# Second attention of a two-layer block: scores in three rounded products, probabilities scaled by GpSimd, one weight's low part later

## The reference

```python
sc = jnp.einsum('bkgqd,bksd->bkgqs', qb, k).astype(jnp.float32) * scale
pr = jax.nn.softmax(sc, axis=-1).astype(v.dtype)
return jnp.einsum('bkgqs,bksd->bkgqd', pr, v)
...
o = o.transpose(1, 0, 4, 2, 3, 5).reshape(b, s, MIX_WIDTH)
return (o * jax.nn.silu(gate)) @ w_out
```

## Time and profile before

| | us |
|---|---|
| median of 3 runs | 1265.69 (1264.97 to 1266.23) |
| profiled execution | 1264.7 |
| its span | 1262.9 |
| PE busy | 1153.4 (91%) |
| DVE busy | 629.2 (50%) |
| ACT busy | 509.6 (40%) |
| POOL busy | 414.4 (33%) |
| mean granted TensorE clock | 0.971 of full |

### The profile page before, as it was taken

How to read it: one execution, slowest core, us unless ns; L and a number is a source line. 1 busy time by engine, 2 the same in 40 slices (tenths; PEclk the granted TensorE clock), 3 DMA queues, 4 the chain that set the end, 5 groups by cost and what they waited for, 6 DMA issues and landing times.

```text
span 1262.9 us, 24765 instructions
## 1 busy us (share of the span) xinstructions
PE 1153.4 (91%) x10379; PEld 971.7 (77%) x10379; DVE 629.2 (50%) x1377; ACT 509.6 (40%) x1038; POOL 414.4 (33%) x214
## 2 busy tenths in 40 slices
PE   3999999999897999999998949987999799999996
PEld 3988887899897998565888949865777678678862
DVE  6000004833647169788246483117865766345546
ACT  4222225842324322788432363144863421132321
POOL 4644374873524344101434234122004441000000
PEclk9999999999899999999998979988999898999999
DMA  7433342232122223100321222431003222100001
GB/s 206 139 101 100 100 130 88 68 87 70 65 68 68 79 90 100 34 2 1 101 81 53 68 100 68 124 118 59 2 1 100 67 67 70 55 31 4 3 3 67
DMA packets 73177, 89.59 MB, mean 71 GB/s; under 512 B 1993, under 2 KB 66634, under 8 KB 72938
## 3 DMA queue, kind: packets, MB, share of 16 engines
q1 hardware_dynamic: 70136, 78.65, 19.5%
q0 software_dynamic: 2416, 8.26, 2.6%
q10 hardware_dynamic: 514, 1.11, 0.4%
HBM read 83.75 MB, written 4.26 MB: 70 GB/s over the span
## 4 chain that ended last, share of the span: by engine, by line
PE 72%; DVE 10%; issue 7%; ACT 5%; POOL 3%; DMA 2%; ACTq 0%; DVEq 0%; POOLq 0%
PE bank L468 67%; PE bank L736 2%; ACT arena L1277 1%; POOL ring_parts L2497 1%; PE bank L902 1%; DMA x<-x_kept 1%; PE bank L646 1%; DVE stat L1776 1%; DVE x L1943 1%; POOL arena L2617 1%; ACT ring_parts L1306 1%; DVE stat L1777 1%; DVE arena L1799 1%; DVE arena L1787 1%; DVE x L1796 1%
## 5 line engine op out<-in xcount | busy, mean ns | idle before, releaser
L2497 POOL TENSOR_TENSOR ring_parts<-ring,ring_parts 128x2048 fp32r<-128x2048 f32 (+1 forms) x59 | 268.4, 4550 | 368.0 <-ACT ring_parts L1306 367.8
L468 PE MATMUL bank<-ring_parts,hT_parts 128*128 128x256 f32 x1664 | 331.6, 285 | 18.9 <-DVE arena_parts L1810 10.8
L468 PE MATMUL bank<-hT_parts,ring_parts 128*128 128x512 f32 x896 | 290.2, 402 | 15.9 <-POOL ring_parts L2497 9.8
L468 PEld LDWEIGHTS bank<-ring_parts,hT_parts 128*128 128x128 f32 x1664 | 270.7, 193 | 20.7 <-issue 11.2
L1277 ACT ACTIVATE arena<-bank 128x512 f32<-128x512 f32 (+3 forms) x356 | 166.7, 527 | 270.7 <-PE bank L468 262.3
L468 PE MATMUL bank<-ring_parts,arena_parts 128*128 128x256 f32 x1088 | 257.0, 285 | 3.4 <-POOL hT_parts L2514 3.4
L468 PE MATMUL bank<-arena 64*64 64x64 f32 (+6 forms) x3440 | 217.6, 276 | 6.5 <-DVE x L2323 2.1
L468 PEld LDWEIGHTS bank<-hT_parts,ring_parts 128*128 128x128 f32 x896 | 173.3, 193 | 58.8 <-POOL ring_parts L2497 11.3
L468 PEld LDWEIGHTS bank<-arena 64*64 64x64 f32 (+2 forms) x3440 | 157.8, 142 | 59.4 <-issue 24.1
L468 PEld LDWEIGHTS bank<-ring_parts,arena_parts 128*128 128x128 f32 x1088 | 190.3, 192 | 4.3 <-POOL hT_parts L2514 3.8
L1306 ACT ACTIVATE ring_parts<-ring 128x2048 fp32r<-128x2048 f32 (+1 forms) x59 | 111.0, 1883 | 80.2 <-PE bank L468 80.2
(11 more groups left out here) (241 smaller groups left out, 1460.7 us busy)
## 6 DMA issues: line engine op xcount, KB each, us to landing
ring<-in_a_w_in SPq DMA_DIRECT2D x16, 1024.0 KB, 5.4
ring<-in_w_in SPq DMA_DIRECT2D x15, 1024.0 KB, 5.5
ring<-in_b_w_in SPq DMA_DIRECT2D x10, 1024.0 KB, 5.1
ring<-in_ple_w_gate SPq DMA_DIRECT2D x8, 1024.0 KB, 4.9
arena<-rpb_rows POOLq DMA_DIRECT2D x16, 256.0 KB, 3.4
ring<-in_a_w_out SPq DMA_DIRECT2D x4, 1024.0 KB, 5.0
ring<-in_b_w_out SPq DMA_DIRECT2D x4, 1024.0 KB, 5.0
ring<-in_w_out SPq DMA_DIRECT2D x4, 1024.0 KB, 5.2
```

What stands on the lines that cost most here:

```text
L468: return nc.tensor.matmul(o, l, r, start=start, stop=stop)
L2497: nc.gpsimd.tensor_tensor(rounded(r), r, read_back(high_slot(n)[:, 0:m]), ALU.subtract)\
```

## The change

- k's and q's transposed tiles become two parts. ScalarE writes the high part (rounded copy, B_high), VectorE then subtracts it from the PSUM bank to get the low part and frees the bank: 12 of them (4 of k, 8 of q). q's low parts go to hT, k's to kTB_lo, new in the arena.
- TensorE turns k's tiles first, then the first halves of q's; the second halves are turned behind scoresB(0), with their parts on ScalarE behind the exponentials of step 0 and on VectorE behind its reciprocals of step 0.
- scoresB issues three rounded products per tile and head, 12 matmuls of 64 rows x 512 columns for a step, the two heads in turn.
- VectorE makes the reciprocals only; GpSimd multiplies the tiles of pB by them (tensor_scalar, B_inverse and B_probs). Its low_pair(1, 0) to (1, 4) stand at the head of steps 6, 8, 10, 12 and 14.
- The low part of the second quarter of the output weights, BO 1, is made behind low_pair(1, 7).

```diff
-        arena = sb2("arena", [P, NARENA], (0, 12288), (19456, 6144))
+        arena = sb2("arena", [P, NARENA], (0, 12288), (19456, 8192))
...
+        kTB_lo = area(25600, 2048).rearrange("p (g t) -> p g t", g=4)
...
 # TensorE
-            for i in range(NT):
-                pe.wait_ge(S("B_rope"), i + 1)
+            def turn_kB(i):
                 pe.wait_ge(S("B_rope_k"), i + 1)
-                for hf in range(2):
-                    b = begin(("BqT", i, hf), "a")
-                    for q in range(4):
-                        o = (4 * hf + q) * P
-                        ins = nc.tensor.transpose(b[:, q * P:(q + 1) * P], qB[:, i, o:o + P], ident)
-                    end(ins)
-                b = begin(("BkT", i), "a")
+                b = begin(("BkT", i), "v")
                 for g in range(4):
                     ins = nc.tensor.transpose(b[:, g * P:(g + 1) * P], kD[:, i, g * P:(g + 1) * P], ident)
                 end(ins)
-            evacuated(pe, ("BkT", NT - 1))
+
+            def turn_qB(i, hf):
+                pe.wait_ge(S("B_rope"), i + 1)
+                b = begin(("BqT", i, hf), "v")
+                for q in range(4):
+                    o = (4 * hf + q) * P
+                    ins = nc.tensor.transpose(b[:, q * P:(q + 1) * P], qB[:, i, o:o + P], ident)
+                end(ins)
+
+            q_parts = [rounded(v[:, :, :]) for v in (qT, hT)]
+            k_parts = [rounded(v[:, :, :]) for v in (kTB, kTB_lo)]
 
             def scoresB(s):
 
-                for m in range(4):
-                    j, i, e = s // 2, 2 * (s % 2) + m // 2, 64 * (m % 2)
-                    b = begin(("BS", 4 * s + m), "a")
-                    end(mm(b[:, :], qT[e:e + 64, j, i * P:(i + 1) * P], kTB[e:e + 64, j // 2, :], True, True))
+                j = s // 2
+                if s == 0:
+                    evacuated(pe, ("BqT", NT - 1, 0))
+                if s == 8:
+                    evacuated(pe, ("BqT", NT - 1, 1))
+                for i in (2 * (s % 2), 2 * (s % 2) + 1):
+                    bs = [begin(("BS", 4 * s + 2 * (i % 2) + e), "a") for e in range(2)]
+                    last = [None, None]
+                    for a, c in ((0, 0), (0, 1), (1, 0)):
+                        for e in range(2):
+                            es = slice(64 * e, 64 * e + 64)
+                            last[e] = mm(bs[e][:, :], q_parts[a][es, j, i * P:(i + 1) * P], k_parts[c][es, j // 2, :],
+                                         (a, c) == (0, 0), a == 1)
+                    for ins in last:
+                        end(ins)
+
+            for i in range(NT):
+                turn_kB(i)
+            for i in range(NT):
+                turn_qB(i, 0)
...
             for s in range(16 + 2):
                 if s < 16:
                     scoresB(s)
+                if s == 0:
+                    for i in range(NT):
+                        turn_qB(i, 1)
 # ScalarE
+            def high_turned(key, dst):
+
+                b = take(act, key)
+                nc.scalar.activation(rounded(dst), b[:, :].rearrange("p (j t) -> p j t", j=4), ACT.Copy)\
+                    .then_inc(S("B_high"), 1)
...
             for i in range(NT):
-                for hf in range(2):
-                    key = ("BqT", i, hf)
-                    b = take(act, key)
-                    give(copy(qT[:, 4 * hf:4 * hf + 4, i * P:(i + 1) * P], b[:, :].rearrange("p (j t) -> p j t", j=4)), key)
-                key = ("BkT", i)
-                b = take(act, key)
-                give(copy(kTB[:, :, i * P:(i + 1) * P], b[:, :].rearrange("p (j t) -> p j t", j=4)), key)
+                high_turned(("BkT", i), kTB[:, :, i * P:(i + 1) * P])
+            for i in range(NT):
+                high_qB(i, 0)
...
+                if s == 0:
+                    for i in range(NT):
+                        high_qB(i, 1)
 # VectorE
+            def low_turned(key, dst, high):
+
+                turned_B[0] += 1
+                dve.wait_ge(S("B_high"), turned_B[0])
+                b = take(dve, key)
+                give(TT(rounded(dst), b[:, :].rearrange("p (j t) -> p j t", j=4), read_back(high), ALU.subtract), key)
...
+            for i in range(NT):
+                ts = slice(i * P, (i + 1) * P)
+                low_turned(("BkT", i), kTB_lo[:, :, ts], kTB[:, :, ts])
+            for i in range(NT):
+                low_qB(i, 0)
...
-                    link(nc.vector.reciprocal(stat[:, c + 8:c + 10], stat[:, c:c + 2]))
-                    for v in (u, u + 1):
-                        c = 144 + v % 8
-                        TS(pB[v % 8], pB[v % 8], stat[:, c:c + 1], None, ALU.mult).then_inc(S("B_probs"), 1)
+                    if u >= 8:
+                        dve.wait_ge(S("B_probs"), u - 6)
+                    nc.vector.reciprocal(stat[:, c + 8:c + 10], stat[:, c:c + 2]).then_inc(S("B_inverse"), 1)
+                if s == 0:
+                    for i in range(NT):
+                        low_qB(i, 1)
 # GpSimd
-                for j in range(2 if l == 0 else 0, 7):
+                for j in range(2 if l == 0 else 5, 7):
                     low_pair(l, j)
...
                 low_pair(l, 7)
+                lower(HI[("AO" if l == 0 else "BO", 1)])
                 if l == 0:
-                    lower(HI[("AO", 1)])
...
-                    lower(HI[("B", 1)], HI[("BO", 1)])
+                    lower(HI[("B", 1)], HI[("BO", 0)])
+                    for s in range(16):
+                        if s >= 6 and s % 2 == 0:
+                            low_pair(1, (s - 6) // 2)
+                        for u in range(4 * s, 4 * s + 4):
+                            pool.wait_ge(S("B_inverse"), u // 2 + 1)
+                            c = 144 + u % 8
+                            nc.gpsimd.tensor_scalar(pB[u % 8], pB[u % 8], stat[:, c:c + 1], None, ALU.mult)\
+                                .then_inc(S("B_probs"), 1)
```

More of the change, by code:

```diff
@@ L1488, in _, with high_qB @@
             high(HI[("BO", 1)])
-            for i in range(NT):
-                for hf in range(2):
-                    key = ("BqT", i, hf)
-                    b = take(act, key)
-                    give(copy(qT[:, 4 * hf:4 * hf + 4, i * P:(i + 1) * P], b[:, :].rearrange("p (j t) -> p j t", j=4)), key)
-                key = ("BkT", i)
-                b = take(act, key)
-                give(copy(kTB[:, :, i * P:(i + 1) * P], b[:, :].rearrange("p (j t) -> p j t", j=4)), key)
+            def high_turned(key, dst):
+                b = take(act, key)
+                nc.scalar.activation(rounded(dst), b[:, :].rearrange("p (j t) -> p j t", j=4), ACT.Copy)\
+                    .then_inc(S("B_high"), 1)
+            def high_qB(i, hf):
+                high_turned(("BqT", i, hf), qT[:, 4 * hf:4 * hf + 4, i * P:(i + 1) * P])
+            for i in range(NT):
+                high_turned(("BkT", i), kTB[:, :, i * P:(i + 1) * P])
+            for i in range(NT):
+                high_qB(i, 0)
             for s in range(16 + 2):
@@ L2021, in _, with low_qB @@
                 gates_B(2 * i + 1)
+            turned_B = [0]
+            def low_turned(key, dst, high):
[3 more added lines that the diff above has]
+                give(TT(rounded(dst), b[:, :].rearrange("p (j t) -> p j t", j=4), read_back(high), ALU.subtract), key)
+            def low_qB(i, hf):
+                at = (slice(None), slice(4 * hf, 4 * hf + 4), slice(i * P, (i + 1) * P))
+                low_turned(("BqT", i, hf), hT[at], qT[at])
+            for i in range(NT):
[3 more added lines that the diff above has]
+                low_qB(i, 0)
             def outB(s):
```

## The result

The changed kernel takes 1288.31 us in the median (1288.01 to 1288.99, 4 runs), the kernel before 1265.96 beside it: ratio 1.0177, 95% interval 1.0159 to 1.0195, 22 us slower. The forecast was 1263.5 us, no change that can be told, with a range of 1259.8 to 1271 us; the measured time lies far above it. The profiled execution took 1288.54 us, its span 1286.4.

A forecast was written before the change was run, and what follows sets the result against it. TensorE was taken to bound the second attention at 5.70 us a step. +1.6 (way in) - 3.8 (12 steps x 0.32) + 0 (way out) = -2.2 us gave 1263.5 us, range 1259.8 to 1271.

The forecast's parts named there:

- the price of GpSimd's scaling: Second attention's steps: one tensor_scalar on 512 columns takes 0.8 us, with 0.54 and 1.28 us as ends.
- rival 2: Second attention: GpSimd becomes the bound or the late one; 1271.5 us at 1.28 per scaling; chance 0.15, half of it slower.
- Products of two heads share the array: Score section of a step: rounded pairs run together, 6 slots of 0.233 us, 1.60 us instead of 1.92.
- The step without GpSimd's bound: Second attention: TensorE's transposes, values and scores, 1.90 + 1.87 + 1.60 = 5.37 us a step, where it was 5.70.
- ScalarE was not next: ScalarE's mean 5.05 us fits the step; the rival that it holds the step near 5.7, 1267.3 us, had chance 0.1.
- The weight's low part: Behind the stage on GpSimd: 4.64 us moved after the last low_pair, with 5 us of cover, costs nothing.
- the low_pairs at the heads of the steps: GpSimd's list in the second attention: five low_pairs, one per second step, adding half of 1.28 us to a step's load.
- The reciprocals never waited for a scaling: VectorE's reciprocals beside GpSimd on the shared port: nothing counted; one that waited would come 0.8 us later.
- The late tiles of the way out: Behind scores(15), waiting for the last scaled tile: no loss at 0.8 us per scaling, 1.2 us at 1.04.
- the way in: From the gates to the end of scores(3): ends at 533.5 instead of 531.88 us, costing 1.6 us.
- over 3 us: Sign against the forecast: it is wrong if the stretch up to scores(3) costs over 3 us.
- the half level of the clock: Start of the second attention: TensorE at 1.2 of 2.4 GHz until about 520 us; one step longer costs 1 us more.

The follow-up runs named there:

- experiment 4: Changed kernel with GpSimd scaling by tensor_tensor, the column repeated with step 0, in place of tensor_scalar: 1263.96 us, ratio 0.9995 to the kernel before.
- experiment 1: Changed kernel with the scaling back on VectorE and the low_pairs in their old place: 1264.20 us, ratio 0.9993 to the kernel before.
- experiment 3: Changed kernel with no scaling at all, so its output is not the block's: 1262.61 us, ratio 0.9984 to the kernel before.
- experiment 9: Kernel before with only the low part of the output weights' second quarter moved behind low_pair(1, 7): 1264.89 us, ratio 1.0004.
- experiment 8: Changed kernel with VectorE scaling and three products of the lower head issued before three of the upper: 1262.11 us, ratio 0.9985 to the kernel before.

## Why the prediction was wrong

**The step that failed** is the price of GpSimd's scaling, and with it the wait that sets the step. The text says "above it the two-input subtraction" and "One input read and one written lies midway between memset and plain: I take 0.8". The argument was that an operation with one input less must be cheaper; it costs 1.565 us against 1.040 (experiment 4). Both ends of the range for it rested on that, so neither was an end, and the weight of rival 2 (0.15, and only up to 1.28 us) was too low. The condition stood there: "it becomes the bound from (5.37 - 0.64)/4 = 1.18 us on". With 1.54 in the place of 0.8 the same sum gives 4 x 1.54 + 0.62 = 6.78 us a step, the measured one. From the first scaling to the last GpSimd's list takes 64 x 1.54 + 5 x 1.24 = 105 us. With 4.4 us from the first scores to the first scaling (518.87 to 523.3) and 4.3 from the last scaling to the last value product (628.4 to 632.7) that is 114 us from the first scores on, where TensorE's stage took 94: 20 of the 20.5 us. The rest is the later start of the scores.

The Trainium skill's "GPSIMD Engine Reference", section "Performance versus the Vector engine", by the estimate of 0.44 to 0.77 us from its figures, points the same wrong way; the measurement of 1.565 decides. Its table "Engine selection" sends elementwise work to VectorE. VectorE does the same tile in 0.44 us, so by the price of one operation the trace agrees; but the same row calls work with one input on GpSimd "roughly line-rate", which 1.565 us doesn't bear out, and with the two-input form the choice of engine made no difference that can be told (experiments 1 and 4).

**What held.** Products of two heads share the array: 1.60 us measured, 1.60 forecast. The step without GpSimd's bound: 5.37, forecast 5.37 (experiments 1, 3 and 4). ScalarE was not next. The weight's low part cost nothing that can be told (experiment 9), and the low_pairs at the heads of the steps didn't hold TensorE once the scaling took 1.04 us (experiment 4). The reciprocals never waited for a scaling: all 32 took 0.150 to 0.168 us in the changed kernel, 0.151 to 0.167 before. The late tiles of the way out cost 1.0 us at a price of 1.04: in experiment 4 from the last scores to the last value product is 11.6 us, 10.6 in experiment 1. The prediction says 1.2, where its own working gives 4 x 0.24 = 1.0.

**A term that was mis-sized:** the way in. From the first scores to the end of scores(3) the forecast had 533.5 - 516.1 = 17.4 us, for 16.4 before. First scores of experiments 1, 3 and 4:

```profile
517.24 0.79 PE L469 MATMUL bank<-arena_parts 64*128 64x512 f32 x2 [4.07 <-DVE hT_parts L2060]
```

```profile
516.13 0.79 PE L469 MATMUL bank<-arena_parts 64*128 64x512 f32 x2 [4.06 <-DVE hT_parts L2060]
```

```profile
519.50 0.79 PE L469 MATMUL bank<-arena_parts 64*128 64x512 f32 x2 [4.07 <-DVE hT_parts L2060]
```

The transposes that end it begin at 537.53, 534.36 and 538.50: 20.3, 18.2 and 19.0 us. The scores also start 0.6 later, as forecast (9.4 us behind the projection's last product in all three, 8.8 before). With that the way in costs 4.5, 2.4 and 3.2 us, not 1.6. The prediction named "over 3 us" as a sign that it is wrong; two of the three are. The 16.4 us before are not a lucky base: experiment 9 has the same way in, runs it at the full clock (1.00 from 512 to 536 us), and takes 16.1.

About 1 us of it is the half level of the clock, held longer than I counted. In the changed kernel the granted clock is 0.50 from 519 to 524 us, the forecast had it back at 520; scores(0) and q's transposes take 2.93 + 3.46 us in the chain above, 2.5 + 2.7 in the forecast. In experiment 1 the clock falls a second time, behind a wait of TensorE of 1.35 us at 528.28:

```profile
530.00:532.00 2.00, 2.00 (x11) 1.31 (x9) 2.00 (x5) 2.00 (x6) 0.00 (x0) 0.50 0.04 8
```

Experiment 3, where nobody scales, has the full clock at this point. Its chain there, against the 1.53 and 2.91 us at 529.63 of experiment 1:

```profile
528.02 0.97 PE bank L469 x6
528.99 1.90 PE bank L755 x16
```

So 1.6 of the 2.1 us by which experiment 1's way in is longer than experiment 3's are the second stretch at the half level. The other 0.5 lie ahead of it, where VectorE's four scalings stand before its low parts.

That is also where the gain went once GpSimd's price is mended: experiment 1: +4.5 - 3.8 = +0.7, experiment 4: +3.2 - 3.8 + 1.0 = +0.4, experiment 3: +2.4 - 3.8 = -1.4 us. The traces' stages agree: 103.4, 103.1 and 101.3 us, against 102.7 before. All three lie within what can be told of the total, or at its edge, as their ratios do. The three rounded products win 0.32 us a step and pay it back in the way in.

**Slips that changed nothing.** The chain before doesn't keep to TensorE from 516 us on: it passes through VectorE between 518.2 and 521.5, and lies on TensorE alone only from 523.06. And the two chances for "faster", 0.18 and 0.14, add up to 0.32, not 0.33.

## What to carry to other kernels

Moving an operation to an engine whose list shows no such operation is a bet on a price, and a form with more inputs isn't a bound from above for it: here tensor_scalar took half as long again as tensor_tensor. When the load is four of them a step, write down the price at which it becomes the bound (1.18 us) and ask what is known to lie under it; only a form that the trace has was known. And a gain per step of 0.3 us over 12 steps must be set against the way into the loop, where the engines wait in a chain and, in these traces, the clock was low.

## What the runs showed of the hardware

- GpSimd, 128 partitions, float32: tensor_scalar 2.5 ns a column + 0.27 us (1.565 at 512, 0.918 at 256; two widths only), with a constant 1.490 at 512; tensor_tensor 1.040 at 512, also where its second input is one column repeated by a step of 0.
- TensorE pairs products on the two row halves although the list has them three apart: all 12 of a step ran in six slots of 0.233 us (experiment 8).
- Rounded products on 64 rows take the same 0.233 us as on 128 rows, two at a time.
